# A hybrid mixer and expert layer: late scan steps scaled on ScalarE, output projection and router interleaved anew

## The chip, the cores and the metric

One core of a Trainium2 chip (trn2). The time is device microseconds of one execution of the whole program. TensorE does matmuls and transposes, VectorE (DVE) and ScalarE (ACT) the elementwise work, POOL and SP mostly issue transfers. Every engine works through its own queue in order, and they meet only at semaphores.

## The reference

One layer over 1024 latent tokens of width 1024, with a prefix of 256 context tokens, all in float32:

```python
h = rms_norm(x, norm_mix_g) * (1 + sc) + sh            # sh, sc, g, sh2, sc2, g2 from the condition c
p = h @ w_in                                            # u | vg | q | o | k | v | gates
y_g = gmlp(u, vg)                                       # chunks of 128 tokens, 4 heads
h_f = mlstm_scan(q, k, v, log_i[0], log_f[0], st_f)     # 8 chunks forward
h_b = mlstm_scan(flipped ...)                           # 8 chunks backward
y_m = sigmoid(o) * head_norm(h_f + h_b, norm_g)
x = x + g * (concat(y_g, y_m) @ w_out)
h2 = rms_norm(x, norm_ffn_g) * (1 + sc2) + sh2
aff = softmax(h2 @ w_router)                            # 16 experts
gate, idx = top_k(aff.T, 128)                           # every expert chooses 128 tokens
x = x + g2 * scatter_add(idx, swiglu_expert(h2[idx]) * gate)
out = rms_norm(x, final_g)
```

In one step of the scan `h_out = num / max(|den|, exp(-m))`; numerator and denominator come out of the same matmuls, as 129 columns for each of four heads. A chunk gets its h from two steps, one in each direction.

## The kernel before, in words

Matmuls with weights run as three products of high and low parts (`mm3`, L1091), to keep float32's accuracy. All stages are written out by hand, one block of code for each engine.

**Scan.** 16 steps, forward and backward in turn (`STEPS`), each on one chunk of 128 tokens. The first eight steps also turn the keys and form the score matrix S (`front`, L1288), which the last eight reuse. TensorE does `front(s + 1)`, then `back(s)` (L1310): the numerators into PSUM banks 4 and 5 and, up to step 13, the update of the state into banks 6 and 7. ScalarE takes the exp `et` (L944) and |den| (L958). VectorE multiplies q by the row factors F (`qs`, L1925) and `et` by S (L1929); then `close_step` (L1849) takes the maximum (L1855) and the reciprocal (L1856), writes h (L1859, the first visit of a chunk) or multiplies and adds it (L1864, the second visit, steps 8 to 15), and updates the state (L1874). `back(s)` waits for `h_done` of the step before, since all numerators share two banks. In the last step ScalarE begins to copy the high halves of `w_out` (`out_high`, L915), and VectorE forms the low ones (`out_low`, L1916).

**Projection and router.** Eight token tiles, in the order `ORDER` in which the scan finishes them. TensorE first multiplies what is ready of tiles 0 to 2 (`out_first`, L1369), turns heads (`head_turn`, L1345, L1353), and ends these tiles (`out_rest`). For the others `out_projection(t)` does 48 matmuls of 512 columns in one go. VectorE normalises heads and gates them (`head_stats`, `head_factors`, `head_gate` L1903, `gated_low` L1909); ScalarE scales them (L927) and copies their high part (`gated_high`, L933). Per tile, VectorE multiplies the sum by g (L1975) into the tile of `h2`, adds x (L1978), and one tile later `normed(t - 1)` (L1959 to L1964) makes h2 of the tile before. ScalarE writes x to `stream`, takes the sum of squares (L999, its target is also `h2`) and the root (L1000), writes h2 to `ffn_in`, and copies the transposed features (`feature_copy`, L987). `to_features` (L1411, L1418) transposes h2 on TensorE into banks 4 and 5. `route` (L1422) multiplies by the router weights, with `wr` (16 columns) loaded and 128 tokens streamed, and lands 16 x 128 logits in bank 7, which ScalarE copies (`logit_copy`, L992); after the last tile eight transposes turn them (L1442). TensorE's order in the loop is: `out_projection(t)`, `head_turn(t + 3)`, `to_features(t - 2)`, `route(t - 2)`. POOL loads x of tile t (L594) once x of tile t - 2 is written and h2 of tile t - 2 is ready.

**Top-k and experts.** VectorE finds the 128 largest of each expert (L1990 to L2027). POOL gathers the tokens of expert 0; `features` (L1453, L1462) transposes them in two halves, both in bank 7, each with a copy (`xeh`, L1025) and a low part (`xel`, L2038), and `expert` (L1466) waits for both. The weights of an expert come through four slots of 2 MB (SP, L692); ScalarE copies each to its high part (L1035), VectorE subtracts (L2058).

Of the kernel before, what the change touches and what calls it, by code (L numbers as in the profile page):

```python
# [6 lines left out]
ALU = mybir.AluOpType  # L7
# [7 lines left out]
P = 128  # L15
# [5 lines left out]
def hybrid_block(nc, x, c, ctx, c_ctx, w_mod, b_mod, norm_mix_g, w_in, conv_q, conv_k, b_igate, b_fgate,  # L21
# [5 lines left out]
    KT = D // P  # L27
# [62 lines left out]
    with es:  # L90
# [146 lines left out]
        qs = wk("qs", [P, 2, H, P])  # L237
        vw = wk("vw", [P, 2, H, V1])
# [14 lines left out]
        lgT = ot("lgT", [NE, NT, P])  # L253
# [6 lines left out]
        topm = ot("topm", [P, NE])  # L260

# [95 lines left out]
        state_up = sem("state_up")  # L357
        hstat_ready = sem("hstat_ready")
# [22 lines left out]
        lg_c = sem("lg_c")  # L381
        lg_t = sem("lg_t")
# [92 lines left out]
        def hbank(n):  # L475

            return 4 + n % 2 if n < 4 else 6


# [9 lines left out]
        def num_view(b):  # L489

            return ps[:, 4 + b, 0:2 * V1].rearrange("p (a v) -> p a v", v=V1)
# [10 lines left out]
        def _(pool):  # L502
# [81 lines left out]
            pool.wait_ge(qs_done, NS)  # L584
            pool.dma_start(wr[:], w_router[0].rearrange("(k p) n -> p k n", p=P)).then_inc(op_in, 16)
# [57 lines left out]
        def _(sp):  # L643
# [71 lines left out]
        def _(act):  # L715
# [220 lines left out]
            for s in range(NS + 1):  # L936
# [17 lines left out]
                if 1 <= s <= NS:  # L954
                    act.wait_ge(num_done, s)
                    if s >= 3:
                        act.wait_ge(h_done, s - 2)
                    act.activation(den[:, (s - 1) % 2, 0, :].rearrange("p (a b) -> p a b", a=2),  # L958
                                   ps[:, 4:6, 0:2 * V1].rearrange("p a (b v) -> p a b v", v=V1)[:, :, :, P],
                                   ACT.Abs).then_inc(abs_done, 1)  # L960
                if 1 <= s <= H:
# [19 lines left out]
            head_scale(4)  # L981

            def feature_copy(t):
# [3 lines left out]
                act.activation(h2T[:, t % 2], two(4, 6).rearrange("p (k t) -> p k t", k=KT),  # L987
                               ACT.Copy).then_inc(h2_c, 1)

            def logit_copy(t):  # L990
                act.wait_ge(rt_done, t + 1)
                act.activation(lgT[:, ORDER[t], :], ps[0:NE, 7, 0:P], ACT.Copy).then_inc(lg_c, 1)  # L992

            for t in range(NT):
# [4 lines left out]
                link(act.activation(h2[:, t % 2], x2[t % 2][:], ACT.Square, accum_out=stat[:, 0, t:t + 1]))  # L999
                act.activation(stat[:, 1, t:t + 1], stat[:, 0, t:t + 1], ACT.Sqrt, bias=epsc[:],  # L1000
                               scale=1.0 / D).then_inc(ss2_ready, 1)
                if t >= 1:
                    act.wait_ge(h2_ready, t)
                    act.dma_start(ffn_in[ORDER[t - 1] * P:(ORDER[t - 1] + 1) * P, :], h2[:, (t - 1) % 2, :]).then_inc(h2_out[(t - 1) % 2], 16)
                    feature_copy(t - 1)
                if t >= 2:
                    logit_copy(t - 2)
                if t + 5 < NT:
                    head_scale(t + 5)
                if t + 3 < NT:  # L1010
                    gated_high(t + 3)
            act.wait_ge(h2_ready, NT)
            act.dma_start(ffn_in[ORDER[NT - 1] * P:(ORDER[NT - 1] + 1) * P, :], h2[:, (NT - 1) % 2, :]).then_inc(h2_out[(NT - 1) % 2], 16)
            logit_copy(NT - 2)
            feature_copy(NT - 1)
            logit_copy(NT - 1)
# [4 lines left out]
            def features_high(e, r):  # L1021
# [3 lines left out]
                act.activation(xeh[:, r * hk:(r + 1) * hk], ps[:, 7, :].rearrange("p (k t) -> p k t", k=hk),  # L1025
# [63 lines left out]
        def _(pe):  # L1089
# [220 lines left out]
            def back(s):  # L1310
# [5 lines left out]
                if s >= 1:  # L1316
                    pe.wait_ge(h_done, s)
                for h in range(H):
                    o = ps[:, 4 + h // 2, h % 2 * V1:(h % 2 + 1) * V1]
# [838 lines left out]
```

## Time and profile before

| | us |
|---|---|
| median of three runs | 1775.42 (1770.96, 1775.42, 1775.69) |
| the profiled execution, own time | 1772.78 |
| its span, first to last instruction | 1771.0 |
| TensorE matmul busy | 1659.1 (94%) |
| VectorE busy | 1354.6 (76%) |
| ScalarE busy | 1039.8 (59%) |
| POOL busy | 146.1 (8%) |

The scan ends near 461 us in the profile's own time, projection and router near 600 us, the top-k near 641 us; the rest are the sixteen experts and the last norm. Busy shares say little about the edited stages, which are chains of short instructions. They are read from the timeline (each instruction with its start, its duration, and in brackets the idle time before it and what ended it) and from the chain of work that ended last. Matmuls overlap: their durations are longer than the distance from one start to the next.

### The profile page before, as it was taken

What the parts mean: (1) busy time and instruction counts of PE and PEld (TensorE: products, weight loads), DVE (VectorE), ACT (ScalarE), POOL (GpSimd) and SP (SyncE); (2) the same over time, 40 slices, a digit from 0 to 9 for tenths busy, and PEclk for the clock granted to TensorE, in tenths of its full rate; (3) what the DMA queues carried; (4) which work ended last, traced back from release to release, by engine and by line L of the source; (5) the groups of instructions that cost most, each with busy time, mean ns of one, the idle gap of its engine ahead of it and who ended that gap; (6) DMA issues with size and microseconds to landing.
All of it is one profiled execution on the core that took longest, in us unless ns stands there. A gap on an engine that the chain in (4) does not pass through costs nothing.

```text
span 1771.0 us, 21856 instructions
## 1 busy us (share of the span) xinstructions
PE 1659.1 (94%) x8224; PEld 1364.7 (77%) x8224; DVE 1354.6 (76%) x1315; ACT 1039.8 (59%) x960; POOL 146.1 (8%) x137
## 2 busy tenths in 40 slices
PE   6999999999989439999999999999999999999995
PEld 2699987879767328888888888888888888888884
DVE  4575543418853578989989999989999899899897
ACT  5252121345432317777777777777777777777775
POOL 3002200002100000101101101101001011011010
PEclk9999999999999759999999999999999999999998
DMA  9116521111223639999999999999999999999996
GB/s 346 60 53 191 176 73 49 48 48 48 86 95 116 241 112 365 365 389 388 370 392 385 368 393 382 371 399 368 388 390 372 384 390 367 389 385 374 393 381 239
DMA packets 204440, 492.81 MB, mean 278 GB/s; under 512 B 5716, under 2 KB 18808, under 8 KB 204392
## 3 DMA queue, kind: packets, MB, share of 16 engines
q1 hardware_dynamic: 187616, 435.30, 66.0%
q0 software_dynamic: 13248, 47.09, 8.8%
q10 hardware_dynamic: 3528, 9.75, 1.4%
q8 instruction: 33, 0.54, 0.1%
q14 instruction: 15, 0.12, 0.0%
HBM read 471.07 MB, written 21.05 MB: 278 GB/s over the span
## 4 chain that ended last, share of the span: by engine, by line
PE 88%; DVE 8%; ACT 2%; DMA 1%; issue 1%; ACTq 0%; DVEq 0%; POOL 0%; POOLq 0%
PE ps L1091 84%; PE ps L1510 2%; PE ps L1462 1%; DVE topi L2008 1%; DVE topv L2007 1%; DVE affT L2010 1%; DMA moda<-in_w_mod 1%; DVE hs L1864 1%; DVE ring L2091 1%; PE ps L1418 0%; PE ps L1110 0%; ACT h2T L987 0%; DVE wl L2058 0%; ACT hs L927 0%; DVE bns L1882 0%
## 5 line engine op out<-in xcount | busy, mean ns | idle before, releaser
L2058 DVE TENSOR_TENSOR wl<-ring,wh 128x2048 fp32r<-128x2048 f32 x384 | 877.5, 2290 | 106.8 <-ACT wh L1035 106.6
L1035 ACT ACTIVATE wh<-ring 128x2048 fp32r<-128x2048 f32 x384 | 737.1, 1921 | 281.5 <-PE ps L1091 281.5
L1091 PE MATMUL ps<-wh,xeh 128*128 128x512 f32 x1024 | 404.9, 395 | 1.4 <-DVE xel L2038 1.4
L1091 PE MATMUL ps<-wh,xel 128*128 128x512 f32 x1024 | 401.7, 392 | 0.0
L1091 PE MATMUL ps<-wl,xeh 128*128 128x512 f32 x1024 | 276.6, 392 | 0.0
L1091 PEld LDWEIGHTS ps<-wh,xeh 128*128 128x128 f32 x1024 | 192.8, 188 | 42.0 <-DVE xel L2038 1.8
L1091 PEld LDWEIGHTS ps<-wh,xel 128*128 128x128 f32 x1024 | 193.0, 189 | 41.5
L1091 PEld LDWEIGHTS ps<-wl,xeh 128*128 128x128 f32 x1024 | 192.5, 188 | 41.7
L1091 PE MATMUL ps<-wh,hidh 128*128 128x512 f32 x512 | 202.7, 396 | 0.0
L1091 PE MATMUL ps<-wh,hidl 128*128 128x512 f32 x512 | 200.1, 391 | 0.0
L1091 PE MATMUL ps<-wl,hidh 128*128 128x512 f32 x512 | 138.3, 392 | 0.0
L612 POOL DMA_INDIRECT stream<-yw,idx_e x15 | 41.7, 2780 | 929.0 <-DVE yw L2048 804.3
L1091 PEld LDWEIGHTS ps<-wl,hidh 128*128 128x128 f32 x512 | 96.2, 188 | 20.7
L1091 PEld LDWEIGHTS ps<-wh,hidl 128*128 128x128 f32 x512 | 96.3, 188 | 20.1
L1091 PEld LDWEIGHTS ps<-wh,hidh 128*128 128x128 f32 x512 | 96.2, 188 | 19.9
L1091 PE MATMUL ps<-hTh,hpl 128*128 128x512 f32 x256 | 100.0, 391 | 0.0
L1091 PE MATMUL ps<-hTl,hph 128*128 128x512 f32 x256 | 99.6, 389 | 0.0
L1091 PE MATMUL ps<-hTh,hph 128*128 128x512 f32 x256 | 99.6, 389 | 0.0
L1091 PE MATMUL ps<-hph,hTl 128*128 128x256 f32 x256 | 73.4, 287 | 0.0
L1091 PE MATMUL ps<-hpl,hTh 128*128 128x256 f32 x256 | 72.4, 283 | 0.0
L1091 PE MATMUL ps<-hph,hTh 128*128 128x256 f32 x256 | 72.4, 283 | 0.0
L1568 DVE TENSOR_TENSOR hpl<-hpr,hph 128x2048 fp32r<-128x2048 f32 x12 | 27.4, 2287 | 38.7 <-ACT hph L755 38.3
(369 smaller groups left out, 2007.9 us busy)
## 6 DMA issues: line engine op xcount, KB each, us to landing
ring<-in_w_gate_e SPq DMA_DIRECT2D x64, 2048.0 KB, 9.3
ring<-in_w_up_e SPq DMA_DIRECT2D x64, 2048.0 KB, 9.0
ring<-in_w_down_e SPq DMA_DIRECT2D x64, 2048.0 KB, 10.7
mbw<-in_w_mod POOLq DMA_DIRECT2D x32, 512.0 KB, 5.1
hpr<-in_w_in SPq DMA_DIRECT2D x12, 1024.0 KB, 5.5
moda<-in_w_mod SPq DMA_DIRECT2D x3, 2048.0 KB, 21.1
xs<-in_x POOLq DMA_DIRECT2D x8, 512.0 KB, 8.6
wor<-in_w_out SPq DMA_DIRECT2D x2, 2048.0 KB, 7.9
```

What stands on the lines that cost most here:

```text
L612: pool.indirect_dma_start(out=stream, out_offset=bass.IndirectOffsetOnAxis(ap=idx_e[:, 1:2], axis=0), in_=yw[:, :], in_offset=None, comput ...
L1035: act.activation(whv[m % 4], eview(m), ACT.Copy).then_inc(hi_done, 1)
L1091: return pe.matmul(o, l, r, start=start, stop=stop)
L1462: last = pe.transpose(ps[:, 7, k * P:(k + 1) * P], xe[:, (r * hk + k) * P:(r * hk + k + 1) * P], ident[:])
L1510: last = pe.transpose(ps[:, 4, k * P:(k + 1) * P], hid[:, q % 2, k * P:(k + 1) * P], ident[:])
L1568: dve.tensor_tensor(hpl[i % 2][:], hpr[i % 2][:], hph[i % 2][:].bitcast(F32), ALU.subtract).then_inc(hp_lo, 1)
L1864: last = dve.scalar_tensor_tensor(out=hs[:, c0, h], in0=num_view(h // 2)[:, h % 2, 0:P], scalar=dn[:, 2, h:h + 1], in1=hs[:, c0, h], op0=A ...
L2007: link(dve.max(topv[:, c8], affT[:]))
L2008: dve.max_index(topi[:, c8], topv[:, c8], affT[:])
L2010: link(dve.match_replace(affT[:], topv[:, c8], affT[:], -1.0))
L2058: dve.tensor_tensor(wlv[m % 4], eview(m), whv[m % 4].bitcast(F32), ALU.subtract).then_inc(lo_done, 1)
L2091: dve.scalar_tensor_tensor(out=finv[:, t, :], in0=finv[:, t, :], scalar=stat[:, 2, t:t + 1], in1=fgrow[:], op0=ALU.mult, op1=ALU.mult).the ...
```

## The change

- In steps 8 to 15 VectorE only makes the reciprocal; ScalarE multiplies the numerators by it into `htmp`, and VectorE adds `htmp` to h one step later (`add_head`). Even late steps put their numerators into banks 0 and 1, odd ones into 4 and 5. POOL's loads for the next stage wait for the last `h_done`.
- `out_projection` is cut into parts, with `to_features` and `route` of the tile before between them; h2 of a tile is made in the same turn as its x. Target tiles of their own take the product with g (`gained`) and the squares (`squares`). Features go to banks 6 and 7, heads from tile 4 on to bank 4, and `route` loads the features (128 columns) and streams `wr` (16 columns), so the logits of all tiles stand in bank 5, turned already. The last tile is added in two halves, a dummy exp stands behind the last root, and `op_done` is counted to 9.
- Expert 0's second half of features has bank 6, and an expert's first matmuls wait for the first half only.

```diff
+        htmp = at(VTR, "htmp", [P, 2, H, P])
...
-        lgT = ot("lgT", [NE, NT, P])
+        gained = at(TAIL + 9280, "gained", [P, D])
+        squares = at(TAIL + 13408, "squares", [P, D])
...
-            return 4 + n % 2 if n < 4 else 6
+            return 4 + n % 2 if n < 4 else 4
+        def fbank(e, r):
+            return 6 if isinstance(e, int) and e == 0 and r == 1 else 7
+        def nbank(s):
+            return 0 if s >= NT and s % 2 == 0 else 4
@@ POOL @@
             pool.wait_ge(qs_done, NS)
+            pool.wait_ge(h_done, NS)
             pool.dma_start(wr[:], ...)
@@ SP @@
-                    sp.wait_ge(op_done, NT)
+                    sp.wait_ge(op_done, NT + 1)
@@ ScalarE @@
+                if s > NT:
+                    if s > NT + 2:
+                        act.wait_ge(h_done, s - 2)
+                    act.wait_ge(rden_ready, s - NT)
+                    for h in range(H):
+                        last = act.activation(htmp[:, s % 2, h], num_view(h // 2, s - 1)[:, h % 2, 0:P], ACT.Copy,
+                                              scale=den[:, (s - 1) % 2, 2, h:h + 1])
+                    last.then_inc(h_scaled, 1)
...
             head_scale(4)
+            gated_high(3)
+            head_scale(5)
...
+            def stream_square(t):
+                act.wait_ge(x2_ready, t + 1)
+                act.dma_start(stream[...], x2[t % 2][:]).then_inc(x2_out[t % 2], 16)
+                if t >= 1:
+                    act.wait_ge(ss2_ready, t)
+                link(act.activation(squares[:], x2[t % 2][:], ACT.Square, accum_out=stat[:, 0, t:t + 1]))
+                act.activation(stat[:, 1, t:t + 1], stat[:, 0, t:t + 1], ACT.Sqrt, ...).then_inc(ss2_ready, 1)
+            for t in range(NT):
+                if t >= 4:
+                    feature_copy(t - 1)
+                stream_square(t)
+                if t < 2:
+                    head_scale(t + 6)
+                    gated_high(t + 4)
+                elif t == 2:
+                    feature_copy(0)
+                    feature_copy(1)
+                elif t == 3:
+                    feature_copy(2)
+                if 3 <= t < 5:
+                    gated_high(t + 3)
+                if t >= 1:
+                    features_out(t - 1)
+            act.activation(stat[:, 3, 0:1], epsc[:], ACT.Exp)
+            features_out(NT - 1)
+            feature_copy(NT - 1)
@@ TensorE @@
-                if s >= 1:
+                if 1 <= s < NT:
                     pe.wait_ge(h_done, s)
+                if s == NT:
+                    pe.wait_ge(sk_c, 2 * NT)
+                if s == NT + 1:
+                    pe.wait_ge(h_done, NT)
+                if s >= NT + 2:
+                    pe.wait_ge(h_scaled, s - NT - 1)
...
+            pe.wait_ge(h_scaled, NT - 1)
             out_first(0, range(H))
-            pe.wait_ge(h_done, NS)
             out_first(1, range(2))
+            pe.wait_ge(h_scaled, NT)
             head_turn(0)
             head_turn(1)
             out_first(1, range(2, H))
             head_turn(2)
+            head_turn(3)
             out_rest(0)
-            head_turn(3)
...
                 for k in range(KT):
-                    last = mm(ps[0:NE, 7, 0:P], wr[:, k, :], h2T[:, t % 2, k], k == 0, k == KT - 1)
+                    last = mm(ps[:, 5, ORDER[t] * NE:(ORDER[t] + 1) * NE], h2T[:, t % 2, k], wr[:, k, :],
+                              k == 0, k == KT - 1)
...
+            for t in range(3, NT):
+                pe.wait_ge(ym_lo, t + 1)
+                pe.wait_ge(op_free, t - 1)
+                half = out_part(t, 0, range(KT))
+                if t == NT - 1:
+                    half.then_inc(op_done, 1)
+                if t == 3:
+                    to_features(0)
+                if t == 4:
+                    route(2)
+                out_part(t, 1, range(H))
+                if t == 3:
+                    route(0)
+                    to_features(1)
+                else:
+                    to_features(t - 1)
+                out_part(t, 1, range(H, KT)).then_inc(op_done, 1)
+                if t == 3:
+                    route(1)
+                    to_features(2)
+                    head_turn(6)
+                else:
+                    if t == 4:
+                        head_turn(7)
+                    route(t - 1)
+            to_features(NT - 1)
+            route(NT - 1)
...
             def expert(e, first, last_one):
-                pe.wait_ge(xel_done, 2 * e + 2)
                 for m in range(2 * EC):
+                    if m < 2:
+                        pe.wait_ge(xel_done, 2 * e + m + 1)
@@ VectorE @@
-                    for h in range(H):
-                        last = dve.scalar_tensor_tensor(out=hs[:, c0, h], in0=num_view(h // 2)[:, h % 2, 0:P],
-                                                        scalar=dn[:, 2, h:h + 1], in1=hs[:, c0, h], ...)
-                    link(last)
-                    dve.nop().then_inc(h_done, 1)
+                    dve.reciprocal(dn[:, 2, :], dn[:, 1, :]).then_inc(rden_ready, 1)
...
+            def add_head(s):
+                c1 = chunk(s)
+                dve.wait_ge(h_scaled, s - NT + 1)
+                dve.tensor_tensor(hs[:, c1], hs[:, c1], htmp[:, (s + 1) % 2], ALU.add).then_inc(h_done, 1)
...
+                if s >= NT + 2:
+                    add_head(s - 2)
...
             head_gate(2)
-            gated_low(2)
             for n in range(4, NT):
                 head_stats(n)
+            gated_low(2)
+            head_gate(3)
+            head_factors(1)
...
+            gated_low(3)
+            def stream_tile(t):
+                c = [slice(0, D)] if t < NT - 1 else [slice(n * W, (n + 1) * W) for n in range(2)]
+                for i, s in enumerate(c):
+                    dve.wait_ge(op_done, t + 1 + i)
+                    if t >= 1:
+                        dve.wait_ge(x2_ready, t)
+                    src = two(obank(t), obank(t) + 2)[:, s]
+                    dve.tensor_tensor(gained[:, s], src, grow[:, s], ALU.mult).then_inc(op_free, 1)
+                    dve.wait_ge(op_free, t + 1 + i)
+                    if i == 0:
+                        dve.wait_ge(x_in[XR + t % 2], ...)
+                    last = dve.tensor_tensor(x2[t % 2][:, s], x2[t % 2][:, s], gained[:, s], ALU.add)
+                last.then_inc(x2_ready, 1)
+            stream_tile(0)
+            head_gate(4)
+            stream_tile(1)
+            gated_low(4)
+            normed(0)
+            head_gate(5)
+            stream_tile(2)
+            normed(1)
+            gated_low(5)
+            normed(2)
+            link(dve.memset(aff[:], 0.0))
+            for t in range(3, NT):
+                stream_tile(t)
+                if t + 3 < NT:
+                    head_gate(t + 3)
+                    gated_low(t + 3)
+                normed(t)
+            dve.wait_ge(rt_done, NT)
```

## Rows read from the trace of the kernel before

**Rows 1.** Waits, 640 to 1771 us: engine line <- awaited: us in total, times, longest
```profile
ACT wh L1035 <- PE ps L1091: 281.5, 376, 5.6
```

**Rows 2.** Timeline of VectorE near 600 us: start, duration, instruction [idle before <- releaser]
```profile
600.82 0.29 DVE L1990 TENSOR_REDUCE srt<-ps 128x8 f32<-128x128 f32 x1
```

**Rows 3.** Timeline of TensorE, first instruction of two steps of the scan
```profile
428.51 0.38 PE L1091 MATMUL ps<-maskb,identb 128*128 128x512 bf16 x1
...
432.16 0.38 PE L1091 MATMUL ps<-maskb,identb 128*128 128x512 bf16 x1
```

**Rows 4.** Timeline of VectorE, late steps of the scan
```profile
452.55 1.13 DVE L1864 SCALAR_TENSOR_TENSOR hs<-ps,den,hs 128x128 f32<-128x128 f32 x4
...
455.46 0.69 DVE L1929 TENSOR_TENSOR et<-et,sS 128x512 f32<-128x512 f32 x1
...
456.63 1.13 DVE L1864 SCALAR_TENSOR_TENSOR hs<-ps,den,hs 128x128 f32<-128x128 f32 x4
```

**Rows 5.** Timelines of ScalarE and TensorE at the end of the scan
```profile
456.01 2.00 ACT L915 ACTIVATE woh<-wor 128x1024 fp32r<-128x1024 f32 x2
...
457.96 0.46 PE L1091 MATMUL ps<-vt,et 128*128 128x129 f32 x2 [2.06 <-DVEq L1868]
...
460.45 0.78 PE L1091 MATMUL ps<-woh,ygTl 128*128 128x512 f32 x1
```

**Rows 6.** Chain that ended last, one tile: start, us, what
```profile
536.31 0.44 PE ps L1353 x4
536.74 0.89 PE ps L1418 x8
...
537.65 1.02 ACT h2T L987
```

**Rows 7.** Timeline of TensorE in the projection and the router
```profile
479.26 0.60 PE L1353 MATMUL ps<-ident,hs 128*128 128x128 f32 x4
...
503.30 1.09 PE L1353 MATMUL ps<-ident,hs 128*128 128x128 f32 x4 [5.52 <-DVE ymT L1903]
...
538.97 1.91 PE L1091 MATMUL ps<-h2T,wr 128*16 128x128 f32 x16 [1.35 <-ACT lgT L992]
540.81 0.50 PE L1091 MATMUL ps<-woh,ygTl 128*128 128x512 f32 x1
...
552.02 1.03 PE L1418 MATMUL ps<-ident,h 128*128 128x128 f32 x8
```

**Rows 8.** Chain that ended last, around the first expert
```profile
650.01 0.70 DVE xel L2038
...
653.35 2.93 PE ps L1091 x6
```

**Rows 9.** ScalarE groups by form, whole span: busy us, mean ns | idle before
```profile
L944 ACT ACTIVATE et<-ps,cols 128x128 f32<-128x128 f32 x64 | 18.3, 372 | 12.6 <-PE ps L1091 12.6
L927 ACT ACTIVATE hs<-hs,mv,rsd 128x128 f32<-128x128 f32 x32 | 13.0, 483 | 0.8 <-DVE mv L1896 0.8
```

**Rows 10.** Timelines of VectorE, POOL, ScalarE; then the landing line of L594
```profile
491.51 1.23 DVE L1978 TENSOR_TENSOR x<-x,h 128x1024 f32<-128x1024 f32 x1
...
499.82 0.16 DVE L1961 RECIPROCAL stat<-stat 128x1 f32<-128x1 f32 x1
...
501.33 1.22 DVE L1964 TENSOR_TENSOR h<-h,b2row 128x1024 f32<-128x1024 f32 x1
...
503.11 0.53 POOL L594 DMA_DIRECT2D x<-in_x  x1 [42.30 <-DVE h L1964]
...
585.42 1.23 DVE L1978 TENSOR_TENSOR x<-x,h 128x1024 f32<-128x1024 f32 x1
...
588.23 0.29 ACT L1000 ACTIVATE stat<-stat,epsc 128x1 f32<-128x1 f32 x1
...
DMA to landing us min/median/max: 4.0/4.4/10.0
```

**Rows 11.** One stretch: us, PE PEld DVE ACT POOL busy, PEclk, DMA, GB/s
```profile
459.00:462.30 3.30, 3.30 (x14) 2.93 (x13) 1.24 (x6) 1.47 (x3) 1.81 (x4) 0.50 0.91 336
```

More of the change, by code:

```diff
@@ L357, in hybrid_block @@
         state_up = sem("state_up")
+        rden_ready = sem("rden_ready")
+        h_scaled = sem("h_scaled")
         hstat_ready = sem("hstat_ready")
@@ L986, in feature_copy @@
                     act.wait_ge(rt_done, t - 1)
-                act.activation(h2T[:, t % 2], two(4, 6).rearrange("p (k t) -> p k t", k=KT),
+                act.activation(h2T[:, t % 2], two(6, 8).rearrange("p (k t) -> p k t", k=KT),
                                ACT.Copy).then_inc(h2_c, 1)
[L990 to L994, printed above, removed]
+            def stream_square(t):
                 act.wait_ge(x2_ready, t + 1)
@@ L1383, in out_rest, with out_part @@
                 last.then_inc(op_done, 1)
-            def out_projection(t):
-                pe.wait_ge(ym_lo, t + 1)
-                pe.wait_ge(op_free, t - 1)
-                for n in range(2):
-                    for k in range(KT):
-                        last = out_product(t, n, k)
-                last.then_inc(op_done, 1)
+            def out_part(t, n, ks):
+                for k in ks:
+                    last = out_product(t, n, k)
+                return last
             pe.wait_ge(yg_lo, H)
@@ L1425, in route @@
                     pe.wait_ge(op_in, 16 * 5)
[L1426 to L1427 removed]
+                    pe.wait_ge(ym_ready, 4)
                 for k in range(KT):
[L1429 removed]
+                    last = mm(ps[:, 5, ORDER[t] * NE:(ORDER[t] + 1) * NE], h2T[:, t % 2, k], wr[:, k, :],
+                              k == 0, k == KT - 1)
                 last.then_inc(rt_done, 1)
[L1432 to L1443 removed]
+            for t in range(3, NT):
[25 more added lines that the diff above has]
+            route(NT - 1)
             pe.wait_ge(aff_ready, 1)
@@ L1939, in _ @@
                     out_low(s - NS + 1)
+            add_head(NS - 1)
+            dve.wait_ge(h_done, NS)
             head_stats(0)
@@ L1969, in _ @@
                                           op1=ALU.mult))
-            for t in range(NT):
-                dve.wait_ge(op_done, t + 1)
-                if t >= 2:
-                    dve.wait_ge(h2_out[t % 2], 16 * (t // 2))
-                    dve.wait_ge(h2_t, t - 1)
-                dve.tensor_tensor(h2[:, t % 2], two(obank(t), obank(t) + 2), grow[:], ALU.mult).then_inc(op_free, 1)
-                dve.wait_ge(x_in[XR + t % 2], 16 * (XS_TURNS[XR + t % 2] + t // 2 + 1))
-                dve.wait_ge(op_free, t + 1)
-                dve.tensor_tensor(x2[t % 2][:], x2[t % 2][:], h2[:, t % 2], ALU.add).then_inc(x2_ready, 1)
-                if t >= 1:
-                    normed(t - 1)
+            gated_low(3)
[9 more added lines that the diff above has]
+                    if i == 0:
+                        dve.wait_ge(x_in[XR + t % 2], 16 * (XS_TURNS[XR + t % 2] + t // 2 + 1))
+                    last = dve.tensor_tensor(x2[t % 2][:, s], x2[t % 2][:, s], gained[:, s], ALU.add)
[13 more added lines that the diff above has]
+                stream_tile(t)
                 if t + 3 < NT:
```

72 lines of the change are left out of this document (21 added, 51 removed).

## The prediction

> **What bounds the kernel now.** I read four views in this order. First the waits of the last 1,130 us, the sixteen experts: in all its stops before a copy of weights ScalarE is held by TensorE and never by a transfer [rows 1]. So this stage is TensorE's; it ends earlier by as much as it starts earlier, and only if its first matmul does. Everything ahead of it is a chain: scan, projection with router, top-k, gather. The top-k takes its logits at 600.82 [rows 2] and is not edited, so what counts is when that row comes, and what happens between the gather and the first expert.
>
> Second, the timeline of the scan. A step without the key work repeats every 3.65 us while h is only written [rows 3] (428.51 to 432.16), with TensorE busy throughout. From step 8 on the period is 4.08 us [rows 4] (452.55 to 456.63), since `back(s)` waits for `h_done` of the step before, and that comes after four multiply-adds of 1.13 us together on VectorE. At the end TensorE stands for 2.06 us before the last numerator [rows 5].
>
> Third, the chain through a projection tile: four transposes of heads, eight of features, then TensorE waits for the 1.02 us copy and a logit copy before it may route [rows 6]: 1.35 us each time [rows 7]. The largest hole is 5.52 us before tile 0's features, where `head_turn(5)` waits for a gate that stands behind `normed(0)` [rows 7].
>
> Fourth, the chain around the first expert: transposes, copy, subtraction, and the same again, since both halves use one bank [rows 8].
>
> **Part 1, late steps.** Removed: four multiply-adds, 1.13 us, a drain of the chain and the `h_done` wait. Added: four ScalarE copies with a scale operand, one VectorE add of 128x512, `h_scaled` and `rden_ready`. The add is priced by the multiply of the same size, 0.69 us [rows 4], so VectorE needs at most 4.08 - 1.13 + 0.69 = 3.64 us a step. The scaled copies do not occur before. The exp with one pointer operand takes 372 ns, four of them 1.14 us; the scaling with two takes 483 ns, four about 1.65 us [rows 9]. One pointer and a PSUM source is the exp's case, so I take 1.14. The loop through ScalarE is then exp 1.14, multiply by S 0.69, maximum and reciprocal 0.45, scaling 1.1, together 3.4 us; with the dearer price it is 3.9. Both banks of numerators alternate, so no reuse wait is on the path, and TensorE's 3.65 us binds. Steps 9 to 14 gain 6 x (4.08 - 3.65) = 2.6 us.
> The Trainium skill ("ScalarE: Activation LUTs", What ACT_TABLE_LOAD costs) gives 93 ns for each pointer operand on top of a base. By it the copy would cost as the exp does; the 111 ns between the two forms of the trace agree roughly, and the sum stays.
>
> Behind the last steps the path changes its owner. The four scaled copies of step 14 now stand ahead of the `woh` copies on ScalarE's queue. Step 14's reciprocal ends at 456.6 - 2.6 = 454.0; scaling to 455.2, half of the 2.00 us `woh` pair [rows 5] to 456.2, the low part 1.2 us to 457.5. There the projection starts, against 460.45 [rows 5]. The 2.06 us wait is thus mostly used up by what is late next. **Gain 2.9 us**, bounds 1.2 (copies at 483 ns, period 3.9) and 3.4.
> Moved besides: POOL waits for the last `h_done` (near 460.4, after the last add) where it waited for the last multiply by F, over by 455.5 [rows 4]. So the router weights, five rows and two x loads go out about 5 us later, and all of POOL's queue with them. The first of them is wanted near 488, so I charge nothing; without this cover it would be those 5 us.
>
> **Part 2, projection and router.** I follow TensorE forward from `head_turn(2)` at 479.26 [rows 7], all other engines in place. Prices: turn 0.44, features 0.89 [rows 6], 48 matmuls 552.02 - 540.81 = 11.21, route 540.81 - 538.97 = 1.84 [rows 7]. The new route streams 16 columns past 128 loaded ones, instead of 128 past 16. No row shows it. Bounds: 16 passes as before (1.84) and half of that, if only the load counts and hides partly. I take 1.84, the row of the same operation.
> - Turns 2 to 5 and three half tiles: 1.8 + 16.8, to 497.9. The gate for turn 5 now stands ahead of `normed(0)`, near 494.4: the 5.52 us hole is gone.
> - VectorE meanwhile: tile 0's x was ready at 492.7 [rows 10]; a gate and a low part, 0.6 each, now stand ahead of it: 493.9. Then a gate 0.6, tile 1 2.5, a wait of some 1.0 for ScalarE's `ymTh`, the low part 0.6 and `normed(0)` 2.73 (499.82 to 502.55, [rows 10]) give h2 of tile 0 at 501.3.
> - **A new wait.** POOL loads tile 2's x after that h2: 0.56 us later, landing 4.4 us after [rows 10], at 506.2. VectorE stands in `stream_tile(2)`, with `normed(1)` queued behind it; ScalarE stands in `stream_square(2)`, with `feature_copy(0)` queued behind. Add 1.23, square and root 1.87 (586.65 to 588.52, [rows 10]), copy 1.07: 510.4. TensorE is through 36 matmuls and tile 0's features at 507.1, and waits 3.3 us.
> - Rest of tile 3: two routes, two features, 12 matmuls, a turn: to 519.1. Tile 4: 11.21 + 0.89 + 0.44 + two routes 3.68, to 535.3. Tiles 5 and 6: 11.21 + 0.89 + 1.84 = 13.9 each, to 563.2. Copies lie under matmuls now: h2 of a tile comes 7.3 us after its `op_done`, its features are due after 8.4 us or more. That margin of 1.1 us is the cover.
> - Tile 7: 12.1, to 575.4. Tail: second half gained and added 1.5, square and root 1.9, `normed` 2.7, features 0.9, copy 1.1, route 1.9: 585.4. No logit copy or transposes. The exp table load lies under `normed(7)`.
> That is 600.8 - 585.4 = 15.4 us. Against it stands TensorE's clock. After its 2.06 us pause it ran 3.30 us at the 1.2 GHz level [rows 11], losing 1.65. After the new 3.3 us wait I charge the same. The last route again follows pauses; at that level it would cost another 1.84, of which I charge half, 0.9. **Gain 12.9 us**, bounds 10 (both clock charges twice) and 22 (none of them, and routes at half).
>
> **Part 3, first expert.** The second half has a bank of its own and m = 0 waits for the first half only. TensorE can start at 650.8, when the first low half ends, against 653.35 [rows 8]: 2.6 us; VectorE's next split moves by 1.5. **Gain 2.3 us**, bounds 1.5 and 2.6. Weight loads start with the second `op_done` of tile 7, over 60 us before use: nothing.
>
> **Sum:** 2.9 + 12.9 + 2.3 = 18.1 us. The profiled execution took 1772.78 (span 1771.0, 1.8 around it), so 1754.7; the median of the three runs is 2.6 higher, so the forecast is 1757.
>
> **Rivals.**
> 1. Late steps stay at about 4 us, because the new loop exp, S, reciprocal, scaling on two engines binds, at 483 ns a copy [rows 9]. For it: ScalarE gains its first real load there. Against: the one-pointer form. 1757 + 2.5 = 1760. Chance 0.10.
> 2. Routes cost half: 8 x 0.9 = 7 less, 1750. For it: only an eighth of the columns stream. Against: transposes with 128 loaded columns come 0.11 us apart, eight in 0.89 [rows 6], and the old route's passes, with 16 loaded, no faster [rows 7]. Chance 0.12.
> The Trainium skill has a rule each way ("TensorE: Matmul & The Clock Gate"): under LDWEIGHTS, a load costs its columns / 1.2 in ns, 107 for 128, which keeps the route at 1.7 us as an estimate and so speaks against this edit; under Back-to-back issue gap, short matmuls come down to some 25 ns. The transposes of this trace, 0.11 us apart, agree with the first, but the columns that they stream explain that as well.
> 3. Tile 2's x lands late: 10.0 us was the longest landing of these loads [rows 10]. Each microsecond passes through VectorE and ScalarE to TensorE: 1757 + 5.6 = 1763. Chance 0.10.
> 4. **Slower than before.** The same place decides: if the load of tile 2's x takes over 4.4 + 18.1 = 22.5 us, the gain is gone; at 30 us it is 1783. For it: both engines' queues stand behind that one load. Against: 4.0 to 10.0 us in eight loads [rows 10]. Chance 0.03.
> 5. The change does not do what it says: the wait merely moves, in the scan to the `woh` copies and in the projection to the tile 3 stop, and under 5 us is left. 1772. Chance 0.05.
>
> The forecast itself has 0.60, own range 1751 to 1763. To hold 8 in 10 with the bounds, and the runs' own spread of 4.7 us, I give 1747 to 1766. A measurement can tell about 0.3%, 5.3 us, from no change: faster 0.92, same 0.05, slower 0.03.
>
> **What would show it.** Late steps 3.65 us apart on TensorE (at 3.9 or more: rival 1). `woh` behind the scaled copies, first projection matmul some 2.9 us earlier. No idle before turn 5; one TensorE wait of about 3.3 us before the first route, behind the copy that stands behind tile 2's x. Routes of 1.8 us with 16 columns (0.9: rival 2). Tiles 5 and 6 13.9 us apart, without waits. The row `srt<-ps` 16 us earlier, counting the scan. First expert matmul 2.6 us after the first transposes begin. The forecast is wrong if a wait of over 1 us a tile shows at features or routes, or if the span from the first expert to the end changes by more than 2 us.

## The result, and the profile after

The changed kernel took 1758.27 us, the median of 4 runs (1754.91 to 1758.55), against 1775.56 for the kernel before in 4 runs beside it (1770.96 to 1775.69). The ratio is 0.9906, with a 95% interval of 0.9894 to 0.9918: faster by 17.3 us between the medians. The profiled execution took 1758.14 us, its span is 1756.3, and the mean granted clock of TensorE is 0.973 (0.977 before).

From here on I compare spans cut at the same six instructions, so that each part of the change has a number of its own. All figures are us, from starts of rows of the timelines. "Upstream" ends with the first exp of the scan, "scan" with the first projection matmul, "projection" with the row `srt<-ps`, "top-k" with the first transposes of the gathered rows, "start" with the first expert matmul.

| kernel | span | upstream | scan | projection | top-k, gather | start | experts |
|---|---|---|---|---|---|---|---|
| before | 1771.0 | 390.79 | 69.66 | 140.37 | 47.35 | 5.18 | 1117.65 |
| after | 1756.3 | 392.80 | 64.86 | 130.65 | 47.46 | 2.59 | 1117.94 |
| difference | -14.7 | +2.01 | -4.80 | -9.72 | +0.11 | -2.59 | +0.29 |

The edit does not touch the upstream stage. In the runs of all variants below it lies between 389.8 and 393.5, so the 2.0 us stand for that spread, which is larger than anything in the other columns that is not edited. The three edited columns give 17.1 us, where the forecast had 2.9 + 12.9 + 2.3 = 18.1. The two profiled executions themselves lie only 14.6 us apart, because of these 2.0 us.

**The late steps.** Timeline of VectorE in the kernel after: one late step with the head of the next, and the end of the last full one, which answers to [rows 4] (start, duration, instruction):
```profile
447.18 0.18 DVE L1912 RECIPROCAL den<-den 128x4 f32<-128x4 f32 x1
447.50 1.12 DVE L1918 SCALAR_TENSOR_TENSOR state<-state,decb,ps 128x129 f32<-128x129 f32 x4
448.54 0.68 DVE L1926 TENSOR_TENSOR hs<-hs,htmp 128x512 f32<-128x512 f32 x1
449.14 0.68 DVE L1975 TENSOR_TENSOR qs<-qT,ps 128x512 f32<-128x512 f32 x1
449.74 0.69 DVE L1979 TENSOR_TENSOR et<-et,sS 128x512 f32<-128x512 f32 x1
450.35 0.15 DVE L1904 TENSOR_TENSOR den<-den,cols 128x4 f32<-128x4 f32 x1
450.53 0.18 DVE L1912 RECIPROCAL den<-den 128x4 f32<-128x4 f32 x1
450.86 1.12 DVE L1918 SCALAR_TENSOR_TENSOR state<-state,decb,ps 128x129 f32<-128x129 f32 x4 [0.15 <-PE ps L1120]
...
453.90 0.18 DVE L1912 RECIPROCAL den<-den 128x4 f32<-128x4 f32 x1
454.00 0.66 DVE L1926 TENSOR_TENSOR hs<-hs,htmp 128x512 f32<-128x512 f32 x1
```
From 447.50 to 450.86 is 3.36 us, where the forecast had 3.65. VectorE looks busy throughout, but it isn't: each state update waits for TensorE. It starts 0.32 or 0.33 us after the reciprocal, where the add at the end, which waits for nothing, starts 0.10 after it. So about 0.22 us of each step is waiting, of which only the 0.15 in brackets is printed, and VectorE's own work is some 3.14 us (an estimate from these rows). TensorE's timeline, in the kernel after and, for [rows 3], in the kernel before:
```profile
446.41 1.06 PE L1120 MATMUL ps<-vw,kn 128*128 128x129 f32 x8
...
447.75 0.40 PE L1120 MATMUL ps<-bdf,sel 128*128 128x512 f32 x1
447.98 0.38 PE L1120 MATMUL ps<-vt,et 128*128 128x129 f32 x2
...
449.77 1.06 PE L1120 MATMUL ps<-vw,kn 128*128 128x129 f32 x8
```
```profile
428.96 0.40 PE L1091 MATMUL ps<-bdf,sel 128*128 128x512 f32 x1
429.40 0.46 PE L1091 MATMUL ps<-vt,et 128*128 128x129 f32 x2
```
TensorE's matmuls for the state update (`vw,kn`) end at 449.77 + 1.06 = 450.83, and VectorE's update starts at 450.86. TensorE itself goes on without a gap: 447.75 to 447.98 is 0.23 us, where the same two rows stand 0.44 apart in the 3.65 us step of the kernel before. So TensorE sets the period in the kernel after, and its own work in a step is 3.36 us. ScalarE's part, from its timeline:
```profile
437.21 1.14 ACT L978 ACTIVATE htmp<-ps,den 128x128 f32<-128x128 f32 x4 [0.52 <-DVE den L1912]
```
Four scaled copies take 1.14 us, about as long as the four exps behind them (1.16), and not 1.65: the forecast's price, and the end of rival 1.

**The end of the scan.** TensorE's timeline, with the first projection matmul, and the windows around it in both kernels (columns as in [rows 11]; the first is of after, the second of before):
```profile
453.84 0.49 PE L1120 MATMUL ps<-vt,et 128*128 128x129 f32 x2 [0.55 <-DVE et L1979]
...
457.66 0.47 PE L1120 MATMUL ps<-woh,ygTl 128*128 128x512 f32 x1 [1.76 <-DVE wol L1966]
```
```profile
458.00:462.00 4.00, 4.00 (x19) 3.32 (x18) 3.93 (x12) 4.00 (x8) 1.27 (x2) 1.00 0.02 4
```
```profile
458.00:462.00 4.00, 4.00 (x20) 3.72 (x21) 1.94 (x5) 1.17 (x4) 2.81 (x6) 0.62 0.83 284
```
The wait of 2.06 us [rows 5] is replaced by 0.55 and 1.76, the second behind the low part of `woh`, which is the change of owner that the forecast names. After these two waits the clock stays at 1.00 (2.4 GHz), where before it fell to 0.50 (1.2 GHz).

**Tile 3 of the projection.** Timelines of VectorE, of ScalarE and of TensorE in the kernel after, where the forecast put its new wait:
```profile
497.61 1.22 DVE L2038 TENSOR_TENSOR gained<-ps,grow 128x1024 f32<-128x1024 f32 x1
502.89 1.23 DVE L2042 TENSOR_TENSOR x<-x,gained 128x1024 f32<-128x1024 f32 x1 [4.06 <-DMA x<-in_x]
```
```profile
504.52 1.06 ACT L1018 ACTIVATE squares<-x 128x1024 f32<-128x1024 f32 x1 [6.16 <-DVE x L2042]
...
505.90 1.00 ACT L1009 ACTIVATE h2T<-ps 128x1024 f32<-128x1024 f32 x1
```
```profile
499.55 1.03 PE L1449 MATMUL ps<-ident,h 128*128 128x128 f32 x8
...
506.96 3.60 PE L1120 MATMUL ps<-wr,h2T 128*128 128x16 f32 x16 [3.62 <-ACT h2T L1009]
...
510.39 1.95 PE L1449 MATMUL ps<-ident,h 128*128 128x128 f32 x8
...
516.78 1.85 PE L1120 MATMUL ps<-wr,h2T 128*128 128x16 f32 x16
...
518.48 1.07 PE L1449 MATMUL ps<-ident,h 128*128 128x128 f32 x8
519.38 0.60 PE L1386 MATMUL ps<-ident,hs 128*128 128x128 f32 x4
```
Read them from top to bottom: VectorE stands for the x of tile 2, ScalarE stands for VectorE with the copy of tile 0's features behind the squares, and TensorE stands 3.62 us for the copy. The forecast had 3.3. What it had too small is in the same fence: the first route takes 3.60 and the transposes 1.95 instead of 1.07. The windows say why:
```profile
506.00:508.00 2.00, 1.04 (x5) 1.04 (x6) 1.96 (x4) 0.91 (x1) 0.50 (x1) 0.50 0.14 57
508.00:510.00 2.00, 2.00 (x11) 2.00 (x11) 1.97 (x2) 0.00 (x0) 0.03 (x1) 0.50 0.50 180
...
512.00:514.00 2.00, 2.00 (x7) 1.61 (x6) 0.00 (x0) 1.02 (x1) 0.00 (x0) 0.50 0.80 295
579.00:590.00 11.00, 5.56 (x24) 5.05 (x24) 3.72 (x7) 3.39 (x5) 0.00 (x0) 0.50 1.02 386
```
TensorE works at 0.50 from the end of its wait through 514, and again in the last 11 us of the tail. From tile 0's features to `head_turn(6)` it is 519.38 - 499.55 = 19.83 us.

**Routes and the tail.** At full clock a route takes 518.48 - 516.78 = 1.70 us, where it was 1.84 [rows 7]. Streaming an eighth of the columns brings 0.14, so rival 2 is out. The Trainium skill ("TensorE: Matmul & The Clock Gate", LDWEIGHTS) has 107 ns for a load of 128 columns, which makes 1.7 us for 16 loads, as an estimate. By that rule, the trace agrees at full clock (0.106 us a pass); at the 1.2 GHz level the same route takes 510.39 - 506.96 = 3.43 us, twice as long, for which that section has no figure. The tail in TensorE's timeline:
```profile
581.60 1.97 PE L1449 MATMUL ps<-ident,h 128*128 128x128 f32 x8 [4.47 <-DVE h L2023]
584.67 3.59 PE L1120 MATMUL ps<-wr,h2T 128*128 128x16 f32 x16 [1.11 <-ACT h2T L1009]
```
Transposes and route there cost nearly double, and both lie on the path to `srt`, at 588.31.

### The profile page after: what moved, and what is told of

It is laid out like the page before. It is cut to its first block, busy times and chain, and to the rows that moved or that the text cites. A ratio compares the mean times of both kernels' runs of the same rounds, so it can differ in the third digit from the quotient of the medians.

```text
span 1756.3 us, 21846 instructions
## 1 busy us (share of the span) xinstructions
PE 1658.2 (94%) x8208; PEld 1371.3 (78%) x8216; DVE 1350.3 (77%) x1293; ACT 1046.6 (60%) x985; POOL 143.9 (8%) x137
## 4 chain that ended last, share of the span: by engine, by line
PE 89%; DVE 6%; ACT 2%; DMA 2%; issue 1%; ACTq 0%; DVEq 0%; POOL 0%; POOLq 0%
PE ps L1120 85%; PE ps L1559 2%; PE ps L1510 1%; DVE topi L2084 1%; DVE topv L2083 1%; DVE affT L2086 1%; DMA moda<-in_w_mod 1%; DVE ring L2167 1%; PE ps L1449 0%; ACT hs L938 0%; PE ps L1139 0%; DVE wl L2134 0%; DVE wol L1966 0%; DVE bns L1932 0%; DMA mbw<-in_w_mod 0%
```

## The experiments

Theory A: the three parts add up, and what the projection lacks against the forecast is TensorE's clock after two waits. Theory B: the parts share one cover, so that one of them alone gives most of the gain. Theory C, for the scan: the second pair of numerator banks brought the shorter steps, not the move to ScalarE. The stages of all runs:

| kernel | span | upstream | scan | projection | top-k, gather | start | experts |
|---|---|---|---|---|---|---|---|
| noscan | 1759.4 | 390.73 | 69.65 | 130.29 | 47.40 | 2.59 | 1118.74 |
| scanonly | 1767.5 | 390.65 | 64.87 | 141.85 | 47.35 | 5.18 | 1117.60 |
| noexp | 1757.6 | 391.05 | 64.87 | 130.57 | 47.91 | 5.18 | 1118.02 |
| banksonly | 1755.6 | 389.84 | 67.22 | 130.66 | 47.50 | 2.59 | 1117.79 |
| copyfirst | 1749.8 | 391.41 | 64.88 | 126.05 | 47.40 | 2.59 | 1117.47 |
| order | 1745.6 | 390.87 | 64.86 | 122.44 | 47.40 | 2.59 | 1117.44 |
| warmroute | 1754.0 | 393.51 | 64.88 | 128.02 | 47.40 | 2.59 | 1117.60 |
| warmtail | 1749.9 | 390.56 | 64.87 | 127.11 | 47.30 | 2.59 | 1117.47 |
| warmgather | 1751.7 | 390.62 | 64.88 | 130.47 | 47.62 | 2.13 | 1115.98 |
| order_warm | 1740.2 | 390.32 | 64.87 | 119.95 | 46.97 | 2.13 | 1115.96 |

**noscan: the change without its scan part.**
```diff
-            return 0 if s >= NT and s % 2 == 0 else 4
+            return 4
...
-                if s >= NT + 2:
-                    pe.wait_ge(h_scaled, s - NT - 1)
...
+                if s >= 1:
+                    pe.wait_ge(h_done, s)
```
and the four multiply-adds in place of the scaled copies and the add.

> The changed kernel with the late scan steps as before (multiply-add on VectorE, one pair of banks); projection, router and first expert stay changed. Theory A (the parts add up, each on the path): the late steps come 4.08 us apart again, first exp to first projection matmul is 69.7 us instead of 64.9, and the time is 4.8 us longer than the changed kernel, near 1763 against 1775.5 of before. Theory B (the scan's gain was mostly taken back behind it, by the woh copies): under 2 us longer, near 1760.

Measured: 1761.44 us (1760.60 to 1762.01), ratio 0.9924, 0.9907 to 0.9941. The scan stage is 69.65, as before the change, and the projection 130.29, as in the kernel after. That second agreement is partly chance: the low clock at the end of the scan is back and costs 1.0 us at the projection's start (first matmul to `head_turn(2)` 18.82 us against 17.81), while tile 3 took 18.46 us instead of 19.83 in this execution, because the clock rose earlier. The stage row puts 4.8 us on the scan part, the medians 3.2.

**scanonly: the kernel before with the scan part alone** (the opposite cut: bank choice, scaled copies, add and waits of the change, and nothing else of it).

> The kernel before with the scan part of the change alone. Theory A: 4.8 us faster than before, ratio near 0.9973, late steps 3.36 us apart, the rest of the stages of their old length. Theory B: under 2 us faster, since the projection starts no earlier behind the woh copies.

Measured: 1769.30 us (1768.82 to 1770.90, 7 runs), ratio 0.9967, 0.9956 to 0.9979. The scan stage is 64.87 again, but in the profiled execution the projection is 1.5 us longer than before. TensorE's timeline, where [rows 7] have routes of 1.91:
```profile
501.27 3.59 PE L1108 MATMUL ps<-h2T,wr 128*16 128x128 f32 x16 [1.11 <-ACT h2T L1004]
504.79 0.80 PE L1108 MATMUL ps<-woh,ygTl 128*128 128x512 f32 x1
```
The large hole of the kernel before is still there, and the low clock behind it covers a route too in this execution. Whether that belongs to the kernel or to the execution isn't shown: how long the clock stays low behind one and the same wait changes from one execution to the next (below), and between the medians scanonly is 1775.67 - 1769.30 = 6.4 us faster than the kernel before, where the stages of the two profiled executions give 3.3. Alone the scan part is thus worth 6.4 us by medians and within the change 3.2, with 4.8 by the stage in both, and the spread of single executions is as large as these differences. In stages the three parts add up, 4.8 + 9.7 + 2.6: theory B falls.

**banksonly: late steps with their own banks, without ScalarE.**
```diff
                 if s >= NT + 2:
-                    pe.wait_ge(h_scaled, s - NT - 1)
+                    pe.wait_ge(h_done, s - 1)
...
+                    for h in range(H):
+                        last = dve.scalar_tensor_tensor(out=hs[:, c0, h], in0=num_view(h // 2, s)[:, h % 2, 0:P],
+                                                        scalar=dn[:, 2, h:h + 1], in1=hs[:, c0, h],
+                                                        op0=ALU.mult, op1=ALU.add)
```

> The changed kernel with the multiply-add of the late steps back on VectorE, but with the two alternating pairs of banks kept (TensorE waits for h of two steps before). Theory A (VectorE's own queue, 4.08 us of work in a step, was the bound; the move to ScalarE is what pays): late steps stay at 3.9 to 4.1 us, first exp to first projection matmul at 67.5 to 69.7 us. Theory B (the wait for h_done of the step before was the bound, as the prediction had it; the banks alone remove it): late steps at 3.65 or less and 66 us or less.

Measured: 1757.44 us in one run, scan 67.22: half of the gain, 2.4 us, is the banks' and half the move's. VectorE's timeline, start of the multiply-adds of two steps:
```profile
434.83 1.13 DVE L1905 SCALAR_TENSOR_TENSOR hs<-ps,den,hs 128x128 f32<-128x128 f32 x4
436.10 1.13 DVE L1915 SCALAR_TENSOR_TENSOR state<-state,decb,ps 128x129 f32<-128x129 f32 x4
...
438.54 0.18 DVE L1897 RECIPROCAL den<-den 128x4 f32<-128x4 f32 x1
438.75 1.13 DVE L1905 SCALAR_TENSOR_TENSOR hs<-ps,den,hs 128x128 f32<-128x128 f32 x4
```
The period is 3.92 us. Here it is VectorE's own queue that sets it: its rows follow each other without a wait, and TensorE stands 0.32 us in every step for VectorE's state update. Six steps of 4.08 - 3.92 give 1.0 us; the other 1.4 come around them, mostly at the end, where the last numerator no longer waits for the old bank (a wait of 1.42 us in place of 2.06) and the clock doesn't fall. The move then takes 0.67 us off VectorE's queue, since the multiply-adds hold it for 1.27 us (434.83 to 436.10) and the add for 0.60 (448.54 to 449.14), and 0.11 more behind the reciprocal (0.21 here, 0.10 in the kernel after). That would make 3.14 us; TensorE's own 3.36 stops the gain at 0.56. Of the 6 x 0.56 = 3.4 us, 0.9 goes back behind the steps: from the reciprocal of step 14 to the first projection matmul it is 457.66 - 453.90 = 3.76 us in the kernel after, where the scaled copies stand ahead of `woh`, and 2.85 in banksonly. Theory C holds for half.

**noexp: the change with both halves of the first expert in one bank.**
```diff
-            return 6 if isinstance(e, int) and e == 0 and r == 1 else 7
+            return 7
```
and the waits of before, with TensorE waiting for both low halves at the expert's head.

> The changed kernel with the first expert's start as before (both feature halves in one bank, a wait for both). Theory A: first transposes of the gathered rows to the first expert matmul 5.2 us instead of 2.6, and 2.6 us slower than the changed kernel. Rival: TensorE is paced by VectorE's splits there, which move by only 1.5 us, and the time is 1.5 us or less slower.

Measured: start 5.18 us against 2.59, with the experts' stage the same within 0.1. From TensorE's timelines, noexp and then after:
```profile
634.40 1.11 PE L1510 MATMUL ps<-ident,xe 128*128 128x128 f32 x4 [8.54 <-DMA xe<-ffn_in,idx_e]
637.08 1.09 PE L1510 MATMUL ps<-ident,xe 128*128 128x128 f32 x4 [1.56 <-DVE xel L2113]
639.58 0.80 PE L1120 MATMUL ps<-wh,xeh 128*128 128x512 f32 x1 [1.41 <-DVE xel L2113]
```
```profile
635.77 1.97 PE L1510 MATMUL ps<-ident,xe 128*128 128x128 f32 x8 [8.11 <-DMA xe<-ffn_in,idx_e]
638.36 0.79 PE L1120 MATMUL ps<-wh,xeh 128*128 128x512 f32 x1 [0.62 <-DVE xel L2114]
```
One round from bank to low half and back goes. The median, 1758.18 (1755.61 to 1759.47), is no different from the change's 1758.27: a part of 2.6 us is lost in a spread of 3.9, and only the stage shows it. That this part is worth 2.6 us is read from the profile alone.

**copyfirst and order: the wait of tile 3 taken away.** Both put the copy of tile 0's features ahead of tile 2's squares on ScalarE; `order` also puts `normed(1)` ahead of `stream_tile(2)` on VectorE. Nothing is added.
```diff
+                if t == 2:
+                    feature_copy(0)
                 stream_square(t)
...
-                    feature_copy(0)
                     feature_copy(1)
...
-            stream_tile(2)
             normed(1)
+            stream_tile(2)
```

> The changed kernel with ScalarE's copy of tile 0's features ahead of the squares of tile 2, and nothing else. The first route no longer waits 3.6 us, but tile 1's features wait for normed(1), which still stands behind tile 2's x on VectorE, until 506.8 in the changed kernel's time, 1.8 us after tile 0's route ends there. Theory A (clock follows the wait): a wait of about 1.8 us and a shorter low stretch, the projection 3 to 5 us shorter than 130.65. Rival (only the copy mattered): as short as with both moves, 122.4.

> The changed kernel with two moves: ScalarE copies tile 0's features before it squares tile 2, and VectorE norms tile 1 before it adds tile 2. Theory A (the 3.6 us TensorE wait comes from two in-order queues behind tile 2's x, and the low clock after it comes from the wait): no wait before the first route, no stretch at clock 0.50 near 506 to 514, 7 to 8 us faster than the changed kernel, near 1750.5. Rival (the wait moves to the features of tile 1 or to tile 3's own x): 3 us or less faster. Rival 2 (the clock falls for another reason): 3.6 us faster, the stretch at 0.50 stays.

Measured: copyfirst 1751.70 us in its one run, projection 126.05; order 1750.31 us (1747.48 to 1752.00), ratio 0.9865, 0.9848 to 0.9881, projection 122.44. TensorE's timeline of order, with a window:
```profile
497.61 1.03 PE L1450 MATMUL ps<-ident,h 128*128 128x128 f32 x8
...
501.23 1.85 PE L1121 MATMUL ps<-wr,h2T 128*128 128x16 f32 x16
502.93 1.07 PE L1450 MATMUL ps<-ident,h 128*128 128x128 f32 x8
...
506.64 1.85 PE L1121 MATMUL ps<-wr,h2T 128*128 128x16 f32 x16
508.34 1.07 PE L1450 MATMUL ps<-ident,h 128*128 128x128 f32 x8
509.24 0.60 PE L1387 MATMUL ps<-ident,hs 128*128 128x128 f32 x4
```
```profile
498.00:508.00 10.00, 10.00 (x67) 8.96 (x66) 7.14 (x9) 3.44 (x5) 1.06 (x2) 1.00 0.64 223
```
No wait and full clock: 509.24 - 497.61 = 11.63 us for the work that took 19.83. Of these 8.2 us, 3.6 were the wait and **4.6 its low clock**. The 4.6 are one execution: in five others that have the same wait there (3.61 to 3.70 us: noscan, noexp, banksonly, warmtail, warmgather), the same work took 18.46 to 19.77 us, so that by the same subtraction the low clock cost 3.2 to 4.5 us. In copyfirst the first route waits for nothing, and a wait of 1.81 us comes at the next features, behind `normed(1)`; the low clock there is over at 509, and the price 3.6 us in all. The x of tile 2 still lands when it does, and VectorE still stands for it, for 1.44 us in order; nothing that TensorE needs soon is queued behind it any longer.

**warmroute and warmtail: the waits kept, TensorE kept at work.** Matmuls of the identity whose results nobody reads are put into the waits: 12 ahead of the first route, and 20 and 3 in the tail.
```diff
+            def warm(bank, n):
+                for i in range(n):
+                    mm(ps[:, bank, i % 4 * P:(i % 4 + 1) * P], ident[:], ident[:], True, True)
...
+                    pe.wait_ge(op_free, 3)
+                    warm(0, 12)
                     route(0)
...
+            pe.wait_ge(op_free, NT - 1)
+            warm(0, 20)
             to_features(NT - 1)
+            warm(0, 3)
             route(NT - 1)
```

> The changed kernel with twelve matmuls of the identity by itself (128 columns, into a free bank) in the wait before the first route; they need 2.7 us of the 3.6. Theory A (the clock loss there, some 4 us, comes from TensorE standing still): no stretch at 0.50 near 506 to 514, the projection 4 us shorter, 126.5, though the copy of the features arrives no earlier. Rival (the matmuls only delay, or the clock falls anyway): 130.7 or more.

> The changed kernel with twenty matmuls of the identity before tile 7's features and three before its route, where TensorE waits 6.2 us and 1.1 us. Theory A: features 0.9 and route 1.8 us instead of 2.0 and 3.6, the projection 2.5 to 2.9 us shorter, near 128. Rival (the chain there is VectorE's and ScalarE's and the matmuls overrun it, or the clock stays low): 130.7 or more.

Measured, one run each: warmroute 1755.97, projection 128.02; warmtail 1751.81, projection 127.11. TensorE in the tail of warmtail:
```profile
573.72 4.71 PE L1120 MATMUL ps<-ident 128*128 128x128 f32 x40
578.34 1.09 PE L1453 MATMUL ps<-ident,h 128*128 128x128 f32 x8
579.27 0.83 PE L1120 MATMUL ps<-ident 128*128 128x128 f32 x6
580.55 1.96 PE L1120 MATMUL ps<-wr,h2T 128*128 128x16 f32 x16 [0.44 <-ACT h2T L1009]
```
The path to these instructions is the same, only the clock differs: 1.09 and 1.96 us for what took 1.97 and 3.59. From the gained half to `srt` it is 582.54 - 572.22 = 10.32 us, against 588.31 - 575.47 = 12.84 in the kernel after: 2.5 us less. The remaining 1.0 of warmtail's 3.5 lies ahead of the tail, which this edit does not touch: at tile 3 the clock fell only during the first route, behind a wait of 3.70 us:
```profile
504.82 2.43 PE L1120 MATMUL ps<-wr,h2T 128*128 128x16 f32 x16 [3.70 <-ACT h2T L1009]
```
It is the spread named above. The tail hardly has such a spread: from the last x to `srt` it takes 12.11 or 12.12 us in every profiled execution of the changed kernel and its variants without filler there, and 9.60 in the two with it. In warmroute the first route runs at 1.96, but the clock falls later, to 0.68 and 0.75 on average from 509 to 515. From tile 0's features to `head_turn(6)` it takes 17.22 us: 2.6 us less than the kernel after, where I expected about 4, but only 1.2 less than noscan, whose wait had no filler. Of the filler at this place one run shows little.

**warmgather and order_warm.** Filler of 20 matmuls, `warm(1, 20)`, stands behind the transposes of the top-k, in the wait for the gather; order_warm is order, warmtail and warmgather together.

> The changed kernel with twenty matmuls of the identity between the top-k's transposes and the gathered rows, where TensorE stands 8.1 us at the low clock. Theory A (the clock follows what TensorE did before): the transposes and the first expert's matmuls run at 1.00, the first expert matmul comes 1.5 us or less after the first transposes instead of 2.6, and the stretch from it to the end is 2 us shorter, 1115.9 instead of 1117.9. Rival (the matmuls overrun the gather, 8.9 us at the low level): the first transposes come up to 1 us later and the rest stays.

> Both moves of the run with the reordered copy and norm, and the identity matmuls in the tail and before the first expert. If the gains are independent: projection 122.4 - 2.9 = 119.5 us, first expert and rest 2.5 us shorter, near 1745, ratio near 0.983 against the kernel before. If the clock losses share a cause with the wait that the moves take away, 1748 or more.

Measured: warmgather 1753.57 us in its one run. Its first expert matmuls take 0.39 to 0.40 us, after 0.50 for the very first, against 0.63 each in the kernel after, and the experts' stage is 2.0 us shorter, at 1115.98 (1115.96 in order_warm; 1117.44 or more in all others). order_warm took 1743.03 us (1742.09 to 1747.11, 5 runs) against 1775.05 (1770.89 to 1776.18, 9 runs), ratio 0.9832, 0.9818 to 0.9846: it beats both kernels, the kernel after by 15 us between the two medians, which were taken on different occasions. Its projection stage of 119.95 is 10.7 under that of the kernel after.

## Why the prediction was right, and where it was short

The time, 1758.27, lies 1.3 us above the forecast of 1757 and in its range. Point by point:

- **Late steps.** The prices held (add 0.69 against 0.69, scaled copies 1.14 against 1.14). The step that failed is "TensorE's 3.65 us binds". The engine was right and its price wrong: TensorE was read as busy throughout at 3.65, but 0.29 of that was short waits that no bracket shows (0.21 of it ahead of the first numerator, which starts at 429.40, right behind VectorE's write of h, over at 429.26: the loop from numerator to `h_done` that the edit cuts); TensorE's own work is 3.36. VectorE's "at most 3.64" was loose too, since it took durations where starts count: from start to start the multiply-adds hold the queue for 1.27 us and not 1.13, the add for 0.60 and not 0.69, and the step of before had 0.16 of waiting in it, as banksonly shows (4.08 against 3.92); VectorE needs some 3.14. With 3.64 as it was stated, VectorE would not have allowed 3.36. Six steps give 4.3 us instead of 2.6, which is nearly all of 4.8 against 2.9. The change of owner to `woh` came, with the wait of 1.76 us that was worked out from the queue.
- **Up to tile 0's features.** `head_turn(2)` to features(0) was forecast at 24.1 and is 499.55 - 475.47 = 24.08; the hole of 5.52 us is gone. Before it 1.0 us came free that was not forecast: without the low clock at the end of the scan, the first projection matmul to `head_turn(2)` takes 17.81 us instead of 479.26 - 460.45 = 18.81.
- **The new wait.** Place, owner and size held: 3.62 against 3.3. The load landed in about 5.2 us instead of 4.4, so rival 3 was true to a small part. What failed is the charge for the clock behind it, "After the new 3.3 us wait I charge the same" (1.65). Features(0) to `head_turn(6)` was forecast at 15.3 before that charge and took 19.83: 4.5 us. The wait of 2.06 us in [rows 11] was one case and no tariff, as the end of the scan shows from the other side, where 0.55 and 1.76 us of waiting cost nothing, and as the 3.2 to 4.6 us behind the same wait in six executions show.
- **Tiles 5 and 6.** 561.55 - 547.75 = 13.80 against 13.9, without waits; all of tiles 4 to 7 come 0.7 us quicker than forecast.
- **Tail.** From the gained half at 575.47 to `srt` at 588.31 it is 12.84 us, where 10.0 and a clock charge of 0.9 were forecast. "Of which I charge half" was the error: both the route and the transposes ran at 1.2 GHz in full, and warmtail, with the clock up, takes 10.32.
- **The projection's sum.** 12.9 - 2.9 (tile 3) - 1.9 (tail) + 0.7 + 1.0 = 9.8, and 9.7 was measured. The clock cost some 7 us in this execution (4.6 by order, 2.5 by warmtail) instead of 2.55.
- **First expert.** 2.59 us against 2.3, and the experts' stage unchanged, as its owner [rows 1] let one expect.

So a term too small in the scan (by 1.9 us), one too large in the projection (by 3.2) and 0.3 at the first expert leave 1.0 us between 18.1 and 17.1. The total was closer than its terms, and one should not take it as proof of them: that the errors cancel is luck. So is part of the 1.3 us at the median, since the forecast put the kernel's profiled execution at 1754.7 and it took 1758.14. Of the rivals, 1, 2, 4 and 5 are out, and 3 is a matter of 0.8 us of landing.

**Left open.** Why the low clock lasted 9 us behind a wait of 3.62 us (matmuls take 0.63 until 515.98 and 0.39 from 516.31), and only some 3 us behind 1.81 and 2.06, isn't settled. The wait's length isn't all of it: the same wait of about 3.6 us cost 3.2 us in noscan and 4.6 in the kernel after, and in warmroute the clock fell later than the wait. The upstream stage's spread of 3.7 us wasn't looked into. No run takes the parts of the new projection one by one, so what the filled hole, the interleaving and the route are worth within its 9.7 us is read from the timelines alone.

## What to carry to other kernels

A wait multiplies when an in-order queue holds something that another engine needs soon behind something that stands for a load: look for that before touching the load, since two swapped lines gave 8.2 us here where the load itself stayed. Charge a wait of TensorE not only its length but also the clock of what follows, and read it from several places and executions, not one. And an engine that looks busy may still be waiting: two engines showed hardly a bracket in the late steps here, and only one of them had no wait. Compare the distance between the same two starts where the engine runs freely, and see whose end the other's start follows.

## What I had not expected of the hardware

A wait of 3.62 us of TensorE was followed by work at 1.2 GHz that cost another 4.6 us, more than the wait itself, and in other executions the same wait cost as little as 3.2. Filler matmuls of the identity in waits that can't be taken away brought 2.5 us in the tail and 2.0 us at the head of the experts, and no delay shows in either place. At 1.2 GHz the route with 16 columns took twice as long, 3.43 us instead of 1.70, although it hardly streams anything. Waits of 0.55 and 1.76 us, with 2.1 us of work between, left the clock at 2.4 GHz, while one of 2.06 us did not.
